# Modulation products summed along rows, and the first part of x ahead of the first weights

## The chip, the cores and the metric

One core of a Trainium2 chip runs the whole program. The metric is the device time of one execution in microseconds (us), the median over runs. TensorE (PE), VectorE (DVE), ScalarE (ACT), GpSimd (POOL) and SyncE (SP) run their own instruction streams and meet only at semaphores. SP and ACT also issue DMAs, each on a queue of its own (q1 is SP's, q10 is ACT's); 16 DMA engines serve both.

## The reference, cut to what matters

Two transformer blocks on 256 tokens of 2048 channels, in fp32. The first is attention, an MLP and a gated embedding. The second is modulated: a vector c (and c_ctx for the context tokens) gives six rows of 2048 that shift, scale and gate its activations.

```python
mod = jax.nn.silu(c) @ w_mod[l] + b_mod[l]          # (2048,) @ (2048, 6 * 2048)
sh_m, sc_m, ga_m, sh_f, sc_f, ga_f = jnp.split(mod, N_MOD)
mod_c = jax.nn.silu(c_ctx) @ w_mod[l] + b_mod[l]     # only its first two parts are used
...
h = modulate(rms_norm_2(x, norm_pre_mix[l]), sh_m, sc_m)    # h * (1 + scale) + shift
```

w_mod is 100 MB; all the other work is matmuls of the 256 tokens with some 490 MB of weights, and attention, a gated scan and convolutions between them.

## The kernel before, in words

**Pieces.** Every weight matrix is cut into pieces of 256 rows by 512 columns, 128 x 1024 in SBUF, 512 KB; there are 940. SP loads a piece into one of four `raw` slots (`load`, L594), ACT rounds it into `whi` (`split`, L695), DVE makes `wlo = raw - whi` (`split`, L1891), and PE does twelve matmuls of 512 columns with it: four each of the tokens' high part with whi, their low part with whi, and their high part with wlo (`chunk`, L1381). Eight pieces are a chunk of 512 output columns (four in two stages). `whi` and `wlo` have four slots each: ACT may split piece p when PE has finished piece p - 4, SP may load into a slot when DVE has made the wlo of the piece that held it. The stages follow one another: "in" (projection, 72 pieces, nine chunks), attention, "o", "ple", "mlp1" (256 pieces), "ctx", "gate", "ctxb", "x2", "gc", "gh", the scan, "pw", "ho", "wo2", "mlp2" (256 pieces).

**Extras.** All other work is put by hand between the pieces: each engine's `chunk` takes a table of extras by slot (0 to 7) of a chunk, and runs an extra before its split of that slot. ACT's and DVE's slots are three pieces ahead of PE. An engine runs its stream in order, so an extra that waits holds the splits behind it.

**Start.** ACT issues the gains and the first part of x (L730 and L731), SP the first piece of weights, then by turns the other three parts of x (`turned_tokens`, L573) and pieces. Each group of x (two of 16 column blocks) is scaled and rounded by ACT (`x_high`, L736) and its low part made by DVE (`x_low`, L1921). PE runs 12 small matmuls on zeros first (`keep_running`, L1448, N_WARM).

**Modulation.** DVE and ACT turn c and c_ctx into silu(c) as columns in `cols`, each value on four partitions (`silu_columns`, L1953, chunk 3 of "in"). Then 192 loads of 512 KB of w_mod come beside the weights (`mod_load`, L631: two DMAs each, into four slots `mraw`), placed by `MOD_PLAN` (L462): 16 in "o", 112 in "mlp1", 32 in "pw" to "wo2", 32 in "mlp2". A load holds 64 rows of w_mod of one part, four partitions to a row. DVE multiplies each half by its column and adds it to `macc` (`mod_product`, L2077; twice where c_ctx counts too). After 32 loads PE transposes `macc` in four 128 x 128 steps (`mod_turn`, L1524; 8 units in all) and DVE sums the result over its free dimension into PSUM (`mod_total`, L2067). `mod_of_mixer`, `other_mods`, `norm4_gain` and `last_mods` add the bias.

**Columns through DRAM.** Where a column vector is wanted as a row on all partitions, ACT writes it to `row_scratch` and reads it back as a broadcast: `lb_columns_out` (L759, chunk 4 of "in", slot 0), `gate_column_out` (L950), and `gate_row_in`, `lb_rows_in` for the reading. In chunks 4 and 5 of "in" SP also loads the attention bias (`two_biases`, L617) in runs of 256 bytes, two DMAs after every piece.

Of the kernel before, what the change touches and what calls it, by code (L numbers as in the profile page):

```python
# [7 lines left out]
ALU = mybir.AluOpType  # L8
# [28 lines left out]
N_WARM = 12  # L37
# [5 lines left out]
        ("norm_post_mix_2", 16), ("norm_post_mlp_2", 16), ("c_2", 64), ("c_ctx_2", 64), ("conv_dw_w_2", 248), ("conv_dw_b_2", 8),  # L43
# [9 lines left out]
ROWS_OF = P // STACK  # L53
# [11 lines left out]
def turned_inputs(a):  # L65

    def by_column(name):
        v = np.asarray(a[name], np.float32).reshape(-1)
        if name in ("c_2", "c_ctx_2"):
            return np.repeat(v.reshape(-1, ROWS_OF).T, STACK, axis=0)  # L70
# [62 lines left out]
def build(nc, I, out):  # L133

    ctx = ExitStack()
    with ctx:
# [50 lines left out]
        c_part = at("c_part", [P, 128], F32, ngain_at)  # L187
# [32 lines left out]
        mraw = at("mraw", [P, MSLOT, 2, NCH], F32, work_at + 40 * K)  # L220
        macc = at("macc", [P, 2, 2, NCH], F32, lev_at)
# [61 lines left out]
        row_scratch = nc.dram_tensor("row_columns", (3, D), F32, kind="Internal").ap()  # L283
        e_scratch = nc.dram_tensor("e_mid", (P, TH, D), F32, kind="Internal").ap()
# [46 lines left out]
        m_red = sem("m_red")  # L331
        m_turned = sem("m_turned")
# [131 lines left out]
        PARTS = [(2, 1), (0, 2), (1, 2), (3, 1), (4, 1), (5, 1)]  # L464
        PART_LOADS = D // (2 * ROWS_OF)
# [26 lines left out]
        MODQ, MOD_AT, SUM_AT, RED_AT = [], {}, {}, {}  # L492
        UNITS, UNIT_END = [], []
        n_ops = 0
        for name, c0, per in MOD_PLAN:
            for a in [8 * (c0 + j) + u for j, count in enumerate(per) for u in AT[count]]:
                m, r = divmod(len(MODQ), PART_LOADS)
                part, nv = PARTS[m]
                MOD_AT.setdefault((name, a // 8), {})[a % 8] = len(MODQ)
                MODQ.append((part, r, m, nv, n_ops))  # L500
                n_ops += 2 * nv
                if r == PART_LOADS - 1:
                    for v in range(nv):
                        at_pe = a + 3 + 2 * v
                        for table, slot in ((SUM_AT, at_pe), (RED_AT, at_pe + 1)):
                            table.setdefault((name, slot // 8), {}).setdefault(slot % 8, []).append(len(UNITS))
                        UNITS.append((m, part, v))
                    UNIT_END.append(len(UNITS))
                    if part == 1:
                        n_ctx_units = len(UNITS)  # L510
            if name == "mlp1":
                n_mlp1_units, n_mlp1_ops, n_mlp1_mods = len(UNITS), n_ops, len(MODQ)
            if name == "mix":
                n_mix_units = len(UNITS)
        assert len(MODQ) == PART_LOADS * len(PARTS)

# [26 lines left out]
        def place(table):  # L543
# [3 lines left out]
            return out  # L547

# [23 lines left out]
        def _(sp):  # L572
# [49 lines left out]

            chunk(w_in, 0, 0, extra={**{u: (lambda u=u: turned_tokens(u + 1)) for u in range(3)}, 6: columns})
# [7 lines left out]
            def mod_load(q):  # L631
                n, r, _, _, _ = MODQ[q]
                if q == n_mlp1_mods:
                    sp.wait_ge(o2_done, NPAIR)
                if q >= MSLOT:
                    done = MODQ[q - MSLOT]
                    sp.wait_ge(m_mul, done[4] + 2 * done[3])
                else:
                    sp.wait_ge(o_lo, NHEAD)
                width = NMOD * D  # L640
# [53 lines left out]
        def _(act):  # L694
# [36 lines left out]
            act.dma_start(xturned[:, 0:2], I["x_turned"][:, 0:2]).then_inc(x_in[0], 16)  # L731
# [19 lines left out]
            def c_exps():  # L751
                act.wait_ge(cols_in, 32)
                nc.scalar.activation(c_part[:], cols[:, COL["c_2"]:COL["c_2"] + 128], ACT.Exp, scale=-1.0).then_inc(c_exp, 1)
# [5 lines left out]
            def lb_columns_out():  # L759
                act.wait_ge(lb_soft, 1)  # L760
                for d in range(2):
                    act.dma_start(row_scratch[2, d * DH:(d + 1) * DH].rearrange("(b p) -> p b", p=P), cols[:, LB0 + 16 * d:LB0 + 16 * d + 8],
                                  allow_slow_non_contiguous=True).then_inc(lb_out, 16)

# [28 lines left out]
            for c in range(IN1 // NCH):  # L793
# [3 lines left out]
                             4: {0: lb_columns_out}}.get(c, {}))  # L797
# [48 lines left out]
            act.dma_start(gbc[:], I["post_mix_norm"][0].partition_broadcast(P)).then_inc(S["gain", "post0"], 16)  # L846
            act.dma_start(pturned[:], I["p_turned"]).then_inc(p_in, 16)
# [91 lines left out]
            mlp("mlp1", 0, True, place({1: high1(3), 2: high1(4), 3: high1(5), 4: high1(6), 5: high1(7), 6: norm1_square,  # L939
# [5 lines left out]
            def lb_rows_in():  # L945
                act.wait_ge(lb_out, 32)
# [17 lines left out]
            def sums_load():  # L964
                act.wait_ge(m_turned, n_mlp1_units)
# [335 lines left out]
            pw_slots = {2: lambda: out_scaled(3), 4: lambda: o2_high(0), 5: lambda: o2_high(1), 7: lambda: o2_high(2), 8: lambda: o2_high(3), 10: lambda: gate_row_in(0, gbc)}  # L1301
# [66 lines left out]
        def _(pe):  # L1368
# [155 lines left out]
            def mod_turn(q):  # L1524
                m, _, v = UNITS[q]
                if q == n_mlp1_units:
                    pe.wait_ge(kt_done, 3 * NPAIR)
                last = MODQ[PART_LOADS * (m + 1) - 1]
                pe.wait_ge(m_mul, last[4] + 2 * last[3])
                if q:  # L1530
                    pe.wait_ge(m_red, q)
# [4 lines left out]
            def sum_inserts(name, c):  # L1536
                return {u: (lambda qs=qs: [mod_turn(q) for q in qs]) for u, qs in SUM_AT.get((name, c), {}).items()}

            p0, g0 = plan["o"]
            for c in range(4):  # L1540
                chunk(p0 + 8 * c, g0 + c, xhi, xlo, inserts=sum_inserts("o", c),
                      tokens={} if c else {u: heads_of(u) for u in range(8)})
# [16 lines left out]
            def mlp(k, u0, extras, first):  # L1559
                p0, g0 = plan[k]  # L1560
                t0 = TG[k][0]
                for i in range(NSB):
                    for j, (kind, c) in enumerate(SEQ):
# [15 lines left out]
                        if k == "mlp2" and n == len(SEQ) * NSB - 1:  # L1579
# [3 lines left out]
                              inserts=merge(extras.get(n, {}), {3: turn_hidden} if j and SEQ[j - 1][0] == "U" else {}, sum_inserts(k, n)),  # L1583
                              tokens=first if n == 0 else {u: hidden(u) for u in range(8)} if kind == "D" and c == 0 else {})
                for f in sum_inserts(k, len(SEQ) * NSB).values():
                    f()
# [264 lines left out]
            for c in range(4):  # L1851
                chunk(p0 + 4 * c, g0 + c, hhi[:, HH:KT], hlo[:, HH:KT], n=4,
                      inserts=merge(slots(ho_slots, 4 * c, 4), mix_slots(SUM_AT, 16 + 4 * c, 4, mod_turn)),
# [7 lines left out]
            chunk(p0, g0, hhi, hlo, inserts=mix_slots(SUM_AT, 32, 8, mod_turn),  # L1861
                  tokens={u: (high_of("y", u), lambda u=u: wo_rest(u)) for u in range(8)})
            for c in range(1, 4):
                chunk(p0 + 8 * c, g0 + c, hhi, hlo, inserts=mix_slots(SUM_AT, 32 + 8 * c, 8, mod_turn))
# [17 lines left out]
        def _(dve):  # L1882
# [70 lines left out]
            def silu_columns():  # L1953
                dve.wait_ge(c_exp, 1)
                cc, ce = cols[:, COL["c_2"]:COL["c_2"] + 128], c_part[:]
# [109 lines left out]
            mps = ps[:, MB, 0:2 * NMOD * KT].rearrange("p (a b) -> p a b", b=2)  # L2065

            def mod_total(q):  # L2067
                _, n, v = UNITS[q]
                dve.wait_ge(m_turned, q + 1)
                to = mps[:, n * KT:(n + 1) * KT, v].rearrange("p (j b) -> p b j", j=STACK)  # L2070
                nc.vector.tensor_reduce(to, ps[:, 7].rearrange("p (b q j) -> p b j q", j=STACK, q=ROWS_OF), AX_X, ALU.add)\
                    .then_inc(m_red, 1)

            def mod_totals(name, c):
                return {u: (lambda qs=qs: [mod_total(q) for q in qs]) for u, qs in RED_AT.get((name, c), {}).items()}

            def mod_product(q):  # L2077
                n, r, m, nv, ops = MODQ[q]
                dve.wait_ge(m_landed[q % MSLOT], 32 * (q // MSLOT + 1))
                if r == 0 and m >= 2:  # L2080

                    dve.wait_ge(m_turned, UNIT_END[m - 2])
                for h in range(2):
                    kt = 2 * r + h
                    for v in range(nv):
                        k = COL["c_2"] + PART_LOADS * 2 * v + kt
                        a, w, x = macc[:, v, m % 2], mraw[:, q % MSLOT, h], cols[:, k:k + 1]
                        if kt == 0:
                            ins = nc.vector.tensor_scalar(a, w, x, None, ALU.mult)
                        else:  # L2090
                            dve.wait_ge(m_mul, ops + nv * (h - 1) + v + 1)
                            ins = nc.vector.scalar_tensor_tensor(out=a, in0=w, scalar=x, in1=a, op0=ALU.mult, op1=ALU.add)  # L2092
# [619 lines left out]
```

## Time and profile before

| | us |
|---|---|
| median of 3 runs | 2819.52 (2816.5 to 2819.88) |
| the profiled execution | 2817.98 |
| its span, first to last instruction | 2816.2 |
| PE busy in the span | 2780.7 (99%) |
| DVE busy | 1996.0 (71%) |
| ACT busy | 1374.8 (49%) |
| DMA, mean over the span | 222 GB/s |

Matmuls are pipelined, so the "mean ns" of one overlaps with the next; the distance from one group of four to the next is what a group costs. Busy time is merged over overlapping instructions. In the profile's rows "<-" after a bracketed time names what ended the idle time before an instruction.

### The profile page before, as it was taken

The numbers are of one execution on the slowest core, as the hardware profiler recorded it, in microseconds if no ns is written. First come the engines' busy times: TensorE is split into PE (matmuls) and PEld (weight loads), VectorE is DVE, ScalarE is ACT, GpSimd is POOL, SyncE is SP. The second block draws the span as 40 slices with busy tenths as digits, with TensorE's granted clock in tenths as the row PEclk, the third lists the DMA queues.
The fourth block names the chain that finished last, engine by engine and source line by source line (L and its number), as shares of the span: only waits on it lengthen the run. The fifth ranks groups of instructions, "written<-read, shape, count | busy, mean of one in ns | idle before, by whom it ended". The sixth has DMA issues, their size and how long they took to land.

```text
span 2816.2 us, 34445 instructions
## 1 busy us (share of the span) xinstructions
PE 2780.7 (99%) x12914; PEld 2312.7 (82%) x12914; DVE 1996.0 (71%) x2265; ACT 1374.8 (49%) x1718; POOL 146.8 (5%) x110
## 2 busy tenths in 40 slices
PE   9999999999999999999999999999989999999998
PEld 7878888888888887788788888898878888888887
DVE  5667877899997676757785488687975467755455
ACT  5446454443444455557444445654564444344443
POOL 0000010010000100000000001000001000010010
PEclk9999999999999999999999999999999999999999
DMA  8963887888888777555666666408856588775654
GB/s 296 208 201 119 278 288 266 276 276 285 284 282 307 255 248 231 194 195 172 216 192 197 197 185 184 133 9 306 304 190 181 193 277 275 255 202 191 190 187 157
DMA packets 332229, 625.23 MB, mean 222 GB/s; under 512 B 36848, under 2 KB 37232, under 8 KB 330224
## 3 DMA queue, kind: packets, MB, share of 16 engines
q1 hardware_dynamic: 323008, 603.41, 67.1%
q10 hardware_dynamic: 9072, 19.83, 2.0%
q8 instruction: 95, 1.56, 0.2%
q14 instruction: 54, 0.44, 0.1%
HBM read 616.83 MB, written 7.27 MB: 222 GB/s over the span
## 4 chain that ended last, share of the span: by engine, by line
PE 91%; DVE 4%; DMA 2%; issue 1%; ACT 1%; SPq 0%; DVEq 0%; POOLq 0%; POOL 0%; ACTq 0%
PE ps L1395 84%; PE ps L1571 1%; DVE wlo L1896 1%; PE ps L1773 1%; DVE macc L2092 1%; PE ps L1374 1%; PE ps L1753 1%; DMA raw<-w_in 1%; DMA raw<-w_o 1%; PE ps L1416 1%; PE ps L1791 1%; PE ps L1496 0%; ACT whi L702 0%; DMA raw<-hgrn_out_w 0%; PE ps L1476 0%
## 5 line engine op out<-in xcount | busy, mean ns | idle before, releaser
L1896 DVE TENSOR_TENSOR wlo<-raw,whi 128x1024 fp32r<-128x1024 f32 x940 | 1169.4, 1250 | 734.2 <-ACT whi L702 729.8
L702 ACT ACTIVATE whi<-raw 128x1024 fp32r<-128x1024 f32 x939 | 994.8, 1060 | 1227.9 <-PE ps L1395 1088.4
L1395 PE MATMUL ps<-whi,hhi 128*128 128x512 f32 x2032 | 549.5, 392 | 0.8 <-DVE yrow L2109 0.8
L1395 PE MATMUL ps<-whi,hlo 128*128 128x512 f32 x2032 | 544.0, 389 | 0.0
L1395 PE MATMUL ps<-wlo,hhi 128*128 128x512 f32 x2032 | 543.4, 389 | 0.5 <-DVE wlo L1896 0.5
L1395 PEld LDWEIGHTS ps<-wlo,hhi 128*128 128x128 f32 x2032 | 381.4, 188 | 80.3 <-DVE wlo L1896 0.9
L1395 PEld LDWEIGHTS ps<-whi,hlo 128*128 128x128 f32 x2032 | 381.1, 188 | 79.6
L1395 PE MATMUL ps<-whi,xhi 128*128 128x512 f32 x1632 | 442.5, 393 | 2.8 <-issue 2.6
L1395 PEld LDWEIGHTS ps<-whi,hhi 128*128 128x128 f32 x2032 | 378.2, 188 | 78.9 <-issue 1.9
L1395 PE MATMUL ps<-whi,xlo 128*128 128x512 f32 x1632 | 439.4, 391 | 0.1
L1395 PE MATMUL ps<-wlo,xhi 128*128 128x512 f32 x1632 | 436.8, 389 | 0.0
L2092 DVE SCALAR_TENSOR_TENSOR macc<-mraw,cols,macc 128x512 f32<-128x512 f32 x504 | 367.3, 760 | 4.6
L1395 PEld LDWEIGHTS ps<-wlo,xhi 128*128 128x128 f32 x1632 | 306.6, 188 | 64.4 <-DVE wlo L1896 0.3
L1395 PEld LDWEIGHTS ps<-whi,xlo 128*128 128x128 f32 x1632 | 306.6, 188 | 64.4 <-DVE xlo L1925 0.5
L1395 PEld LDWEIGHTS ps<-whi,xhi 128*128 128x128 f32 x1632 | 304.3, 189 | 64.8 <-issue 3.2
L2631 POOL TENSOR_TENSOR sqrow<-rrow 128x512 f32<-128x512 f32 x64 | 93.1, 1475 | 1153.6 <-ACT rrow L898 1153.6
L2339 DVE SCALAR_TENSOR_TENSOR yT<-uT,cols,yT 128x252 f32<-128x252 f32 (+17 forms) x144 | 53.1, 437 | 0.0
L2611 POOL TENSOR_TENSOR stat<-stat 128x2 f32<-128x2 f32 x9 | 9.8, 1086 | 656.1 <-DVE stat L2098 441.9
L2157 DVE TENSOR_TENSOR hlo<-ps,hhi 128x512 fp32r<-128x512 f32 x64 | 41.0, 682 | 0.0
L1212 ACT ACTIVATE dec<-ps 128x1024 f32<-128x1024 f32 x32 | 32.5, 1023 | 17.2 <-PE ps L1753 10.8
L1773 PE MATMUL ps<-qD,kD 128*128 128x128 f32 x256 | 34.7, 279 | 3.6 <-DVE qD L2415 2.1
L1773 PEld LDWEIGHTS ps<-qD,kD 128*128 128x128 f32 x256 | 31.0, 192 | 5.1 <-DVE qD L2415 3.1
(303 smaller groups left out, 1470.6 us busy)
## 6 DMA issues: line engine op xcount, KB each, us to landing
raw<-w_in SPq DMA_DIRECT2D x296, 512.0 KB, 4.4
raw<-mlp_w SPq DMA_DIRECT2D x256, 512.0 KB, 4.1
mraw<-w_mod SPq DMA_DIRECT2D x384, 256.0 KB, 5.0
raw<-w_up SPq DMA_DIRECT2D x128, 512.0 KB, 4.7
raw<-w_down SPq DMA_DIRECT2D x128, 512.0 KB, 5.0
raw<-w_o SPq DMA_DIRECT2D x32, 512.0 KB, 5.5
raw<-w_ple_gate SPq DMA_DIRECT2D x32, 512.0 KB, 3.8
raw<-w_out SPq DMA_DIRECT2D x32, 512.0 KB, 5.8
```

The source lines that it names most:

```text
L702: nc.scalar.activation(whi[:, s % NSLOT], raw[:, s % NSLOT], ACT.Copy).then_inc(hi_done, 1)
L1212: nc.scalar.activation(dst, src, ACT.Exp).then_inc(d_done, 1)
L1374: ins = nc.tensor.transpose(ps[:, TB[t % 2], c:c + P], src, ident)
L1395: ins = nc.tensor.matmul(ps[:, bank(par) + th], a[:, kt, th * P:(th + 1) * P], b[:, (s + u) % NSLOT, k], start=(kt == 0 and m == 0), stop= ...
L1416: ins = nc.tensor.matmul(ps[:, bank(g) + th], a[:, kt, th * P:(th + 1) * P], b[:, u % NSLOT, k], start=kt == 0 and m == 0, stop=kt == KT - ...
L1571: ins = nc.tensor.transpose(ps[:, TB[(t0 + h) % 2], a * T + th * P:a * T + (th + 1) * P], sqrow[:, th, f:f + P], ident)
L1773: ins = nc.tensor.matmul(o[:, (2 * hh + n) * P:(2 * hh + n + 1) * P], k[:, hh, n * P:(n + 1) * P], q[:, hh, t * P:(t + 1) * P], start=True ...
L1896: nc.vector.tensor_tensor(wlo[:, s % NSLOT], raw[:, s % NSLOT], whi[:, s % NSLOT].bitcast(F32), ALU.subtract)\
L2092: ins = nc.vector.scalar_tensor_tensor(out=a, in0=w, scalar=x, in1=a, op0=ALU.mult, op1=ALU.add)
L2157: nc.vector.tensor_tensor(hlo[:, kt:kt + 2], ps[:, TB[(t0 + h) % 2]].rearrange("p (a b) -> p a b", a=2), hhi[:, kt:kt + 2].bitcast(F32), A ...
L2339: nc.vector.scalar_tensor_tensor(out=y, in0=tap_part(uT[:, ct], ct, dd, True), scalar=wcol(TAPS // 2 + dd, ct), in1=y, op0=ALU.mult, op1=A ...
L2631: nc.gpsimd.tensor_tensor(sqrow[:, th], rrow[:, th], rrow[:, th], ALU.mult).then_inc(sq_done, 1)
```

## The change

The host passes w_mod transposed (`w_mod_turned`, 12288 x 2048), so a tile holds 128 outputs on the partitions and 1024 of the 2048 inputs along the row. `silu_rows_out` writes silu(c) and silu(c_ctx) from their columns to a DRAM tensor `silu_rows`; `silu_rows_in` broadcasts halves of these rows onto all partitions (`crows`, two slots, exchanged in five phases). DVE's product of a tile with a row is one `tensor_tensor_reduce` whose sum lands in a column of `msum`; the two halves are added later (`mod_parts`). The transposes on PE and the sums of them on DVE are gone. The 192 loads stay at the same places, one DMA each. c and c_ctx come as 16 columns each instead of 64. The first part of x is issued by SP ahead of the first weights, and N_WARM is 11.

```diff
-N_WARM = 12
+N_WARM = 11
...
-        macc = at("macc", [P, 2, 2, NCH], F32, lev_at)
+        mraw = at("mraw", [P, MSLOT, D // 2], F32, work_at + 40 * K)
+        crows = at("crows", [P, 2, D // 2], F32, lev_at)
+        msum = at("msum", [P, 2, (NMOD + 2) * KT], F32, lev_at + 8 * K)
...
+        TILES = [[(2, n, h, 1) for n in range(KT) for h in range(2)],
+                 [(part, n, 0, 2) for part in (0, 1) for n in range(KT)],
+                 [(part, n, 1, 2) for part in (0, 1) for n in range(KT)],
+                 [(3, n, h, 1) for n in range(KT) for h in range(2)],
+                 [(part, n, h, 1) for part in (4, 5) for n in range(KT) for h in range(2)]]
+        CROWS_LOADS = [[(0, 0), (0, 1)], [(1, 0)], [(1, 1), (0, 1)], [(0, 0)], [(0, 0), (0, 1)]]
...  SyncE
+            turned_tokens(0)
             chunk(w_in, 0, 0, extra={**{u: (lambda u=u: turned_tokens(u + 1)) for u in range(3)}, 6: columns})
...
-                for h in range(2):
-                    src = bass.AP(I["w_mod_2"].tensor, ROWS_OF * (2 * r + h) * width + n * D, [[width, ROWS_OF], [NCH, STACK], [1, NCH]])
-                    sp.dma_start(mraw[:, q % MSLOT, h], src).then_inc(m_landed[q % MSLOT], 16)
+                src = I["w_mod_turned"][part * D + n * P:part * D + (n + 1) * P, h * (D // 2):(h + 1) * (D // 2)]
+                sp.dma_start(mraw[:, q % MSLOT], src).then_inc(m_landed[q % MSLOT], 16)
...  ScalarE
-            act.dma_start(xturned[:, 0:2], I["x_turned"][:, 0:2]).then_inc(x_in[0], 16)
...
+            def silu_rows_out():
+                act.wait_ge(silu_done, 1)
+                for v in range(2):
+                    act.dma_start(silu_rows[v].rearrange("(b p) -> p b", p=P), cols[:, COL["c_2"] + v * KT:COL["c_2"] + (v + 1) * KT],
+                                  allow_slow_non_contiguous=True).then_inc(lb_out, 16)
+
+            def silu_rows_in(phase):
+                if phase:
+                    act.wait_ge(m_mul, PHASE_FIRST[phase][1])
+                else:
+                    act.wait_ge(lb_out, 64)
+                for v, h in CROWS_LOADS[phase]:
+                    act.dma_start(crows[:, CROWS_HOLD[phase][v, h]], silu_rows[v, h * (D // 2):(h + 1) * (D // 2)].partition_broadcast(P))\
...
-                             4: {0: lb_columns_out}}.get(c, {}))
+                             4: {0: lb_columns_out, 1: silu_rows_out}}.get(c, {}))
...
             act.dma_start(gbc[:], I["post_mix_norm"][0].partition_broadcast(P)).then_inc(S["gain", "post0"], 16)
+            silu_rows_in(0)
...
+            pw_slots = {1: last_silu_rows, 2: lambda: out_scaled(3), ...
...  TensorE
-            def mod_turn(q):
...
-                for b in range(4):
-                    ins = nc.tensor.transpose(ps[:, 7, b * P:(b + 1) * P], macc[:, v, m % 2, b * P:(b + 1) * P], ident)
-                ins.then_inc(m_turned, 1)
...  VectorE
+                if q == PHASE_FIRST[phase][0]:
+                    dve.wait_ge(crows_in, 16 * sum(len(x) for x in CROWS_LOADS[:phase + 1]))
+                dve.wait_ge(m_landed[q % MSLOT], 16 * (q // MSLOT + 1))
+                w = mraw[:, q % MSLOT]
+                for v in range(nv):
+                    k = (NMOD if v else part) * KT + (part * KT if v else 0) + n
+                    product = w if v == nv - 1 else ps[:, MB:MB + 2].rearrange("p a b -> p (a b)")
+                    if v:
+                        dve.wait_ge(m_mul, ops + v)
+                    nc.vector.tensor_tensor_reduce(out=product, in0=w, in1=crows[:, CROWS_HOLD[phase][v, h]], scale=1.0, scalar=0.0,
+                                                   op0=ALU.mult, op1=ALU.add, accum_out=msum[:, h, k:k + 1]).then_inc(m_mul, 1)
+
+            def mod_parts(dst, a, b, bias):
+                step(nc.vector.tensor_tensor(dst, msum[:, 0, a:b], msum[:, 1, a:b], ALU.add))
+                return nc.vector.tensor_tensor(dst, dst, bias, ALU.add)
```

## Rows read from the trace of the kernel before

**Rows 1.** Busy time by stretch (span, engines, PE clock, DMA share, GB/s).
```profile
0.00:20.00 20.00, 17.78 (x74) 14.41 (x75) 11.04 (x17) 11.68 (x20) 0.57 (x10) 1.00 0.92 331
20.00:210.00 190.00, 188.63 (x845) 155.90 (x844) 118.13 (x133) 91.34 (x104) 8.93 (x5) 1.00 0.84 227
350.00:1070.00 720.00, 720.00 (x3277) 597.60 (x3276) 608.30 (x701) 335.37 (x373) 47.47 (x34) 1.00 0.82 275
1900.00:2005.00 105.00, 104.54 (x488) 86.35 (x487) 87.74 (x97) 45.47 (x59) 1.41 (x1) 1.00 0.87 304
```

**Rows 2.** Waits of PE: who waited for whom, total, times, longest.
```profile
PE ps L1395 <- DVE yrow L2109: 0.8, 1, 0.8
```

**Rows 3.** Groups by line on PE: the transposes of the modulation.
```profile
L1533 PE MATMUL ps<-small,macc 128*128 128x128 f32 x32 | 4.8, 272 | 0.0
```

**Rows 4.** Timeline of PE around one unit: start, duration, instructions.
```profile
1068.98 1.07 PE L1395 MATMUL ps<-whi,hlo 128*128 128x512 f32 x4
1069.88 1.07 PE L1395 MATMUL ps<-wlo,hhi 128*128 128x512 f32 x4
1072.15 1.08 PE L1395 MATMUL ps<-whi,xlo 128*128 128x512 f32 x4
```

**Rows 5.** Groups by line on DVE.
```profile
L2092 DVE SCALAR_TENSOR_TENSOR macc<-mraw,cols,macc 128x512 f32<-128x512 f32 x504 | 367.3, 760 | 4.6
L1932 DVE CUSTOM_DVE_ANT_0 xjunk<-res 128x2048 f32<-128x2048 f32 x1 | 2.3, 2287 | 0.0
```

**Rows 6.** DMA issues of the span: count, KB each, median us to landing.
```profile
gbc<-post_mix_norm ACTq DMA_DIRECT2D x1, 1024.0 KB, 4.6
row_columns<-cols ACTq DMA_DIRECT2D x2, 4.0 KB, 12.1
row_columns<-mcol ACTq DMA_DIRECT2D x2, 8.0 KB, 12.5
```

**Rows 7.** Timeline of the start, ACT and PE.
```profile
6.51 1.71 ACT L740 ACTIVATE xhi<-xturned,cols 128x256 fp32r<-128x256 f32 x4 [3.31 <-DMA xturned<-x_turned]
7.51 1.17 PE L1395 MATMUL ps<-whi,xhi 128*128 128x512 f32 x4 [1.04 <-issue]
14.44 1.06 ACT L702 ACTIVATE whi<-raw 128x1024 fp32r<-128x1024 f32 x1 [2.78 <-DMA raw<-w_in]
16.35 0.77 PEld L1395 LDWEIGHTS ps<-whi,xhi 128*128 128x128 f32 x4 [0.57 <-ACT xhi L740]
17.60 0.77 PEld L1395 LDWEIGHTS ps<-whi,xlo 128*128 128x128 f32 x4 [0.48 <-DVE xlo L1925]
```

**Rows 8.** DMA, 1093 to 1107, in 40 slices; SP's queue: packets, MB, share.
```profile
GB/s 304 117 47 21 7 7 6 0 6 0 0 29 12 18 6 146 29 18 18 53 29 23 29 23 29 35 18 35 35 18 6 41 23 23 59 152 199 228 257 222
q1 hardware_dynamic: 417, 0.80, 54.8%
```

**Rows 9.** DMA, 96 to 108, in 40 slices.
```profile
GB/s 239 198 190 130 137 172 321 333 300 221 170 196 123 70 63 9 0 0 8 0 6 9 16 18 36 6 4 40 37 33 13 36 22 60 76 55 79 180 146 90
```

**Rows 10.** Timeline of ACT in the second MLP.
```profile
2504.84 1.06 ACT L702 ACTIVATE whi<-raw 128x1024 fp32r<-128x1024 f32 x1 [5.79 <-DMA raw<-mlp_w]
```

**Rows 11.** Timeline of ACT in the projection stage.
```profile
95.95 1.03 ACTq L762 DMA_DIRECT2D row_columns<-cols  x2
107.24 1.06 ACT L702 ACTIVATE whi<-raw 128x1024 fp32r<-128x1024 f32 x1 [4.74 <-DMA raw<-w_in]
129.60 1.06 ACT L702 ACTIVATE whi<-raw 128x1024 fp32r<-128x1024 f32 x1 [1.66 <-DMA raw<-w_in]
```

**Rows 12.** Timeline of PE in the projection stage.
```profile
131.11 1.07 PE L1395 MATMUL ps<-whi,xhi 128*128 128x512 f32 x4
```

**Rows 13.** Timeline of PE after a wait.
```profile
1128.41 1.08 PE L1374 MATMUL ps<-small,res 128*128 128x128 f32 x4 [4.34 <-DVE hlo L1914]
1133.84 1.09 PE L1395 MATMUL ps<-whi,xhi 128*128 128x512 f32 x4
```

**Rows 14.** Timeline of SP in the projection stage.
```profile
102.00 8.10 SPq L615 DMA_DIRECT2D bm<-bias_rows  x2
```

More of the change, by code:

```diff
@@ L490, in build @@
         n_pieces = pc[0]
-        MODQ, MOD_AT, SUM_AT, RED_AT = [], {}, {}, {}
-        UNITS, UNIT_END = [], []
+        MODQ, MOD_AT = [], {}
+        PHASE_FIRST, PHASE_AT = [], []
+        order = [(phase, tile) for phase, tiles in enumerate(TILES) for tile in tiles]
         n_ops = 0
@@ L496, in build @@
             for a in [8 * (c0 + j) + u for j, count in enumerate(per) for u in AT[count]]:
-                m, r = divmod(len(MODQ), PART_LOADS)
-                part, nv = PARTS[m]
+                phase, (part, n, h, nv) = order[len(MODQ)]
+                if phase == len(PHASE_FIRST):
+                    PHASE_FIRST.append((len(MODQ), n_ops))
+                    PHASE_AT.append((name, a))
                 MOD_AT.setdefault((name, a // 8), {})[a % 8] = len(MODQ)
[L500 to L510, printed above, removed]
+                MODQ.append((phase, part, n, h, nv, n_ops))
+                n_ops += nv
+                last_at = a
+                if (part, n, h) == (1, KT - 1, 1):
+                    n_ctx_ops = n_ops
+                if len(MODQ) < len(order) and order[len(MODQ)][0] != phase:
+                    PHASE_AT[phase] += (last_at,)
             if name == "mlp1":
-                n_mlp1_units, n_mlp1_ops, n_mlp1_mods = len(UNITS), n_ops, len(MODQ)
+                n_mlp1_ops, n_mlp1_mods = n_ops, len(MODQ)
             if name == "mix":
-                n_mix_units = len(UNITS)
-        assert len(MODQ) == PART_LOADS * len(PARTS)
+                n_mix_ops = n_ops
+        assert len(MODQ) == len(order) and [name for name, *_ in PHASE_AT] == ["o", "mlp1", "mlp1", "mlp1", "mix"]
         TURN_U = 4
@@ L547, in place, with merge_places @@
             return out
+        def merge_places(*tables):
+            return {c: merge(*[place(t).get(c, {}) for t in tables]) for c in {a // 8 for t in tables for a in t}}
         def slots(table, first, n=8):
@@ L631, in mod_load @@
             def mod_load(q):
-                n, r, _, _, _ = MODQ[q]
+                _, part, n, h, _, _ = MODQ[q]
                 if q == n_mlp1_mods:
@@ L1522, in heads_of @@
                 return (lambda: pe.wait_ge(o_hi, n)), (lambda: pe.wait_ge(o_lo, n))
-            def mod_turn(q):
[L1525 to L1531, printed above, removed]
-                for b in range(4):
-                    ins = nc.tensor.transpose(ps[:, 7, b * P:(b + 1) * P], macc[:, v, m % 2, b * P:(b + 1) * P], ident)
-                ins.then_inc(m_turned, 1)
-            def sum_inserts(name, c):
-                return {u: (lambda qs=qs: [mod_turn(q) for q in qs]) for u, qs in SUM_AT.get((name, c), {}).items()}
             p0, g0 = plan["o"]
             for c in range(4):
-                chunk(p0 + 8 * c, g0 + c, xhi, xlo, inserts=sum_inserts("o", c),
-                      tokens={} if c else {u: heads_of(u) for u in range(8)})
+                chunk(p0 + 8 * c, g0 + c, xhi, xlo, tokens={} if c else {u: heads_of(u) for u in range(8)})
             def turn1(g):
@@ L1860, in wo_rest @@
                 pe.wait_ge(t_free, TG["y"][0] + u + 1)
-            chunk(p0, g0, hhi, hlo, inserts=mix_slots(SUM_AT, 32, 8, mod_turn),
-                  tokens={u: (high_of("y", u), lambda u=u: wo_rest(u)) for u in range(8)})
+            chunk(p0, g0, hhi, hlo, tokens={u: (high_of("y", u), lambda u=u: wo_rest(u)) for u in range(8)})
             for c in range(1, 4):
-                chunk(p0 + 8 * c, g0 + c, hhi, hlo, inserts=mix_slots(SUM_AT, 32 + 8 * c, 8, mod_turn))
+                chunk(p0 + 8 * c, g0 + c, hhi, hlo)
             def norm4_turn(g):
@@ L2064, in _ @@
             dve.wait_ge(silu_done, 1)
[L2065 to L2075, printed above, removed]
@@ L2077, in mod_product @@
-            def mod_product(q):
[L2078 to L2092, printed above, removed]
-                        ins.then_inc(m_mul, 1)
+            def mod_product(q):
+                phase, part, n, h, nv, ops = MODQ[q]
+                if q == PHASE_FIRST[phase][0]:
[9 more added lines that the diff above has]
+                                                   op0=ALU.mult, op1=ALU.add, accum_out=msum[:, h, k:k + 1]).then_inc(m_mul, 1)
@@ L2187, in other_mods @@
             def other_mods():
-                for f in mod_totals("mlp1", len(SEQ) * NSB).values():
-                    f()
-                dve.wait_ge(m_red, n_mlp1_units)
-                nc.vector.tensor_tensor(modT[:, NX:NP], mps[:, NX:NP, 0], bmod[:, NX:NP], ALU.add).then_inc(mod_out, 1)
+                dve.wait_ge(m_mul, n_mlp1_ops)
+                mod_parts(modT[:, NX:NP], NX, NP, bmod[:, NX:NP]).then_inc(mod_out, 1)
             def other_gains():
@@ L2198, in norm4_gain @@
             def norm4_gain():
-                dve.wait_ge(m_red, n_mix_units)
-                step(nc.vector.tensor_tensor(modT[:, NP:NM], mps[:, NP:NM, 0], bmod[:, NP:NM], ALU.add))
+                dve.wait_ge(m_mul, n_mix_ops)
+                step(mod_parts(modT[:, NP:NM], NP, NM, bmod[:, NP:NM]))
                 mod_gain(2, 4, 0, "norm_pre_mlp_2")
@@ L2491, in f @@
                             nc.vector.tensor_tensor(add_to[:, :, s], add_to[:, :, s], dst[:, :, s], ALU.add).then_inc(merged, 1)
-                    chunk(p0 + 4 * c, f, n=4, extra=merge(slots(extras, 4 * c, 4), mix_slots(RED_AT, first + 4 * c, 4, mod_total),
+                    chunk(p0 + 4 * c, f, n=4, extra=merge(slots(extras, 4 * c, 4),
                                                           mix_slots(MOD_AT, first + 4 * c, 4, mod_product)))
@@ L2548, in _ @@
             for c in range(4):
-                chunk(p0 + 8 * c, lambda c=c: post3_gain(c), extra=merge(slots(wo_slots, 8 * c), mix_slots(RED_AT, 32 + 8 * c, 8, mod_total),
+                chunk(p0 + 8 * c, lambda c=c: post3_gain(c), extra=merge(slots(wo_slots, 8 * c),
                                                                                              mix_slots(MOD_AT, 32 + 8 * c, 8, mod_product)))
@@ L2556, in last_mods @@
             def last_mods():
-                dve.wait_ge(m_red, len(UNITS))
-                step(nc.vector.tensor_tensor(modT[:, NM:], mps[:, NM:, 0], bmod[:, NM:], ALU.add))
+                dve.wait_ge(m_mul, n_ops)
+                step(mod_parts(modT[:, NM:], NM, NMOD * KT, bmod[:, NM:]))
                 nc.vector.tensor_tensor(mcol[:, 4], modT[:, NM:], col("norm_post_mlp_2"), ALU.mult).then_inc(mcol_done, 1)
@@ L2704 @@
     arrays.update(turned_inputs(arrays))
+    del arrays["w_mod_2"]
     arrays.update(shape_constants())
```

55 lines of the change are left out of this document (27 added, 28 removed).

## The prediction

> **What bounds the kernel now.** I read the table of busy time by stage first: PE is busy 188.63 of 190 us in the projection stage (20 to 210), 720 of 720 in 350 to 1070 and 104.54 of 105 in 1900 to 2005 [rows 1]. The waits of PE come next; the only one near the modulation work is 0.8 us for DVE's last evacuation of the output projection [rows 2]. So PE's own instructions set the end. Time saved on DVE, ACT or SP is worth nothing unless PE waited for it; a PE instruction taken out is worth its own time; and weights that come later than PE's lookahead cost one for one. A piece goes through raw, whi and wlo with four slots each, so ACT splits a piece three pieces before PE uses it. The third reading is therefore DMA: its share is 0.84 in the projection stage, 0.82 in the first MLP and 0.87 in 1900 to 2005 [rows 1].
>
> **Transposes out.** The trace has 32 of them, eight units of four [rows 3]. Four matmuls of 512 columns follow one another at 0.90 us (1068.98 to 1069.88). With one unit between, two such steps took 2.27 us (1069.88 to 1072.15) instead of 1.81 [rows 4]. A unit is worth 0.46 us, eight are worth 3.7 us, all in stages where PE is full: -3.7.
>
> **Products along the row.** DVE now does 504 steps of 760 ns and 8 cheaper first ones. After the change it does 256 multiply-and-sums of 1024 columns. One such over 2048 columns took 2287 ns [rows 5]; half of it, 1.1 to 1.2 us, is my estimate, against 1.5 us for the two steps it replaces, or some 70 us of DVE in all. PE hardly waits for DVE, so this is worth at most the 0.8 us of [rows 2], with nothing as the other end. SP also issues one DMA per load instead of two. I take -0.4, the middle.
>
> **Rows of silu(c) into SBUF.** These are eight broadcasts of 512 KB. A broadcast of 1024 KB landed in 4.6 us [rows 6]. The first two are issued when attention ends, and the first product is a chunk of eight pieces later (8 x 2.72 = 21.8 us, by the step of [rows 4]): no cost. In the first MLP the rows are exchanged three times. ACT issues the load once DVE has finished the products that read the old rows, and the next product is three slots later once and two slots (5.4 us) later twice. There DVE waits perhaps 3 to 6 us for the landing, and behind it in DVE's queue stand the next wlo splits, for which PE waits. PE is three pieces (8.2 us) ahead, so two exchanges should pass; the one that loads two rows at once, with two products per tile after it, may not. Bounds 0 and +4, taken +1, near the lower end since the lookahead covers most. The last two loads (1 MB) come just before the busy stretch at 1900; at its 304 GB/s [rows 1] they are 3.4 us of transfer. Bounds 0 and +3.4; they start before the modulation loads of that stretch, and SP and DVE have less to do there, so I take 0.
>
> **First part of x first.** The first real matmul starts at 7.51 us, and what it waits for is x: ACT was idle 3.31 us for it. But PE then waits again at 16.35 and 17.60, since the fourth piece of weights landed only for the split at 14.44 (ACT idle 2.78 us for it), and the fourth group of x is cast behind that split [rows 7]. The order of the other transfers and their bytes are unchanged, and DMA is full (share 0.92 over the first 20 us, [rows 1]). So PE would start earlier, by 1 us perhaps, and lose it at the fourth piece. Bounds -1 (all of it kept) and +0.5 (one more issue of 0.47 us ahead of that piece); I take 0. One warm-up matmul less lies in the same idle stretch.
>
> **The rows written to DRAM.** This is the term that decides. silu_rows_out writes two vectors, partition by partition: 2048 separate elements of 4 bytes each. The kernel has this shape already: gate_column_out writes one 8 KB vector so, and lb_columns_out two halves of 4 KB. They take 12.5 and 12.1 us to land, where 1024 KB in long runs took 4.6 [rows 6]. What they do to the weights is the point. In the stretch with one 8 KB write, all traffic drops to 26 GB/s on average over 33 slices of 0.35 us (the third to the 35th), 11.5 us, one of them above 60 [rows 8]. In the stretch with the two halves it is 29 GB/s over 24 slices of 0.3 us (the 14th to the 37th), 7.2 us [rows 9]. A 2048-element write thus stops the weights for 7.2 to 11.5 us. Before the change one comes alone: in the second MLP ACT then idles 5.79 us for weights [rows 10] and PE does not wait, as the lookahead takes it.
> After the change three come in a row in the projection stage: lb_columns_out at slot 0 of chunk 4, and two more at slot 1. The first alone uses up the reserve. Issued at 95.95, it makes the split at 107.24 wait 4.74 us, and from there to 129.60 seven pieces come at 3.19 us each, slower than PE's 2.72, because the attention bias is being read in small runs [rows 11]. PE starts on the piece that is split at 129.60 at 131.11 [rows 12]; its split ends at 130.66, so the reserve left is 0.45 us. Two more writes block 2 x 7.2 = 14.4 to 2 x 11.5 = 23 us; middle 19. In that time some 26 GB/s still pass, 0.49 MB, about one piece, worth 3 us. The weights shift by 16, PE stalls by 16 - 0.45 = 15.5. Ends: 14.4 - 3 - 0.5 = +11 and 23 - 3 = +20. After the stop PE must also restart: after one wait of 4.34 us a unit of transposes and twelve matmuls took 5.43 us (1128.41 to 1133.84) instead of 0.46 + 2.72 [rows 13], so 2.2 us; while weights come slower than PE uses them some of this is hidden, taken +1.
> A rule of the Trainium skill speaks against this term. The page "DMA: Bandwidth & Descriptors", section "Queues, rings and completion order", says that each DMA engine takes turns between the queues that have work, a packet at a time. By it the weights on SP's queue would keep every second turn beside ACT's element writes, and the sum would be that of the first rival below. The trace does not agree: the weights' queue moved 0.80 MB in the 14 us of [rows 8].
>
> **Sum.** The profiled execution took 2817.98 us (span 2816.2 and 1.78 around it). 2817.98 - 3.7 - 0.4 + 1 + 0 + 15.5 + 1 = 2831.4, forecast 2831. The median of the three runs shown, 2819.52, lies 1.5 us above the profiled execution; that is inside the range.
>
> **Rivals.**
> (1) The element writes share. The weights keep enough turns beside them, and the lookahead covers the rest as it does in the second MLP [rows 10]. Then the sum without the 15.5 and the restart holds: 2817.98 - 3.7 - 0.4 + 1 = 2814.9, between 2811 and 2818: not slower. It decides if the two added writes together delay the splits by under about half a microsecond, or if they run beside the first at the same total of 12 us. For it: only one case of a lone write with a busy weight queue is shown to cost PE nothing. Against: both GB/s rows.
> (2) ACT is held at the issue. SP once stood 8.10 us over the issue of two small DMAs while the element write ran [rows 14]. If ACT stands likewise behind its first 2048 elements, it can't split pieces that have landed already, raw slots are not freed, and weight loads start late when the block ends: a landing of 4.6 us and one split more, about +7: 2838, 2835 to 2844.
> (3) Half the block. The writes to rows of DRAM overlap each other, and two cost what one costs: 9.5 - 3 - 0.5 = 6 in place of 15.5, so 2822, 2818 to 2825: no measurable change or a little slower.
> (4) The change does not do what it says at the start: the first matmul is not earlier, as x and the first weights now share one queue. It moves the sum by nothing, since the fourth piece decides either way.
>
> **Chances.** Forecast 0.70 (its own range 2825 to 2840), rival 1 0.14, rival 2 0.08, rival 3 0.08. A measurement of this kernel can tell about 0.2% (5.6 us) from no change. Faster by more (under 2813.9): 0.06, less than half of rival 1. Within: 0.17, the rest of rival 1, nearly all of rival 3, and a forecast with every term at its cheap end. Slower: 0.77. The range of 2814 to 2841 leaves out some 0.06 below and 0.08 above.
>
> **What would show it.** Right: in the projection stage PE busy falls by some 15 us, its longest waits there go to wlo or whi and from there to raw<-w_in, DMA's traffic stays under 80 GB/s for some 25 to 30 us from 97 on, the two silu_rows writes land more than 20 us after their issue, and everything behind the stage runs as before, eight units of 0.46 us shorter. The first matmul starts earlier and PE waits longer at the fourth piece. Wrong: the two writes landing within some 12 us of their issue, PE busy all through 95 to 140, or waits of PE on DVE at the exchanges of rows in the first MLP that add up to more than the stage at the start.

## The result, and the profile after

The changed kernel takes 2833.57 us (median of 5 runs, 2832.41 to 2835.08) against 2818.50 us for the kernel before beside it (5 runs, 2816.50 to 2819.88). The ratio is 1.0053, with a 95% interval of 1.0042 to 1.0063: slower by half a percent, which is small but clear of the noise. The profiled execution has a span of 2831.8 us.

Busy time in the first three of the four stretches of [rows 1], now in the changed kernel (columns as there):

```profile
0.00:20.00 20.00, 17.57 (x74) 14.52 (x75) 11.41 (x17) 12.23 (x20) 0.57 (x10) 1.00 0.91 330
20.00:210.00 190.00, 179.22 (x769) 147.30 (x768) 110.32 (x126) 82.39 (x92) 8.03 (x5) 0.96 0.89 212
350.00:1070.00 720.00, 719.75 (x3269) 596.79 (x3268) 586.04 (x707) 338.63 (x384) 56.68 (x35) 1.00 0.82 278
```

Only the projection stage (20 to 210) differs much: PE is busy 179.22 us of 190 instead of 188.63, its clock 0.96 instead of 1.00. The waits of PE name the releaser (total, times, longest):

```profile
PE ps L1420 <- ACT whi L706: 11.2, 3, 5.8
PE ps L1399 <- ACT xs L1362: 6.5, 1, 6.5
PE ps L1399 <- DVE hlo L1920: 4.6, 1, 4.6
```

The second and third line stood in the kernel before too; the first is new, and 10.8 us of it, two waits, lie in the projection stage. ACT's timeline around it (start, duration, instructions, the idle time ahead of them and its releaser) says why the splits are late:

```profile
95.58 1.03 ACTq L765 DMA_DIRECT2D row_columns<-cols  x2
96.74 13.41 ACTq L771 DMA_DIRECT2D silu_rows<-cols  x2
110.25 3.90 ACT L706 ACTIVATE whi<-raw 128x1024 fp32r<-128x1024 f32 x4 [12.46 <-issue]
129.30 1.06 ACT L706 ACTIVATE whi<-raw 128x1024 fp32r<-128x1024 f32 x1 [15.16 <-DMA raw<-w_in]
132.56 1.06 ACT L706 ACTIVATE whi<-raw 128x1024 fp32r<-128x1024 f32 x1 [2.20 <-DMA raw<-w_in]
```

First ACT is held 13.41 us while it issues the two element writes (its idle 12.46 us end with the issue, and four splits follow at once); then it waits 15.16 us for weights. The DMA view of 95 to 137 (40 slices of 1.05 us; then packets, MB and share of the queues of SP and of ACT) shows the stop, and the list of DMA issues the landing:

```profile
GB/s 311 111 257 216 61 12 10 19 27 14 41 89 208 196 52 11 11 4 0 3 22 45 39 35 45 33 62 55 66 26 63 98 140 272 334 219 299 233 262 248
q1 hardware_dynamic: 5564, 4.41, 78.5%
q10 hardware_dynamic: 6208, 0.02, 38.8%
silu_rows<-cols ACTq DMA_DIRECT2D x2, 8.0 KB, 26.3
```

From the fifth slice to the thirty-first, 28 us, three slices are above 80 GB/s: they carry the bytes of about one piece of weights (0.52 MB). Two pieces that were issued at 95.26 and 99.15 land in the stop, 11.9 and 13.0 us later; the next one lands only at 129.3. PE's timeline gives the whole loss, if it is read from start to start, four matmuls being 0.907 us where nothing is late (the groups in between are left out):

```profile
105.35 1.07 PE L1420 MATMUL ps<-wlo,xhi 128*128 128x512 f32 x4
111.36 2.07 PE L1420 MATMUL ps<-whi,xhi 128*128 128x512 f32 x4 [4.94 <-ACT whi L706]
116.25 1.07 PE L1420 MATMUL ps<-whi,xhi 128*128 128x512 f32 x4
123.51 1.07 PE L1420 MATMUL ps<-wlo,xhi 128*128 128x512 f32 x4
130.41 2.08 PE L1420 MATMUL ps<-whi,xhi 128*128 128x512 f32 x4 [5.84 <-ACT whi L706]
136.89 1.07 PE L1420 MATMUL ps<-whi,xlo 128*128 128x512 f32 x4
```

The first wait costs 6.01 - 0.91 = 5.10 us and the slow restart (4.89 us for three groups, instead of 2.72) 2.17; the second wait 6.90 - 0.91 = 5.99 and its restart (6.48 us for four groups instead of 3.63) 2.85. Together 16.1 us. In the slow groups four matmuls take 1.7 to 1.9 us. The granted clock is 0.50, the lower level (1.2 GHz), from 111.4 to 114.9 and from 130.4 to 135.7, behind each wait, and 1.00 from 117 to 123 in between.

Where else the time moved can be read by the start of the same product in each trace against the kernel before (in us; a negative figure is earlier; pieces are counted over the whole program):

| start of | changed | rows in runs (e1) | start alone (e5) |
|---|---|---|---|
| first product | -1.2 | -0.8 | -1.1 |
| piece 8 to 30, projection | -0.4 | 0.0 | 0.0 |
| piece 48, projection | +15.8 | 0.0 | 0.0 |
| first MLP, start | +15.2 | -0.5 | +0.5 |
| context, start | +12.9 | -3.0 | +0.5 |
| after the context products | +13.2 | -4.2 | 0.0 |
| middle of the second block's input | +14.3 | -3.4 | +0.6 |
| after the scan | +16.0 | -2.0 | +2.1 |
| second MLP, piece 5 | +15.8 | -2.3 | +2.4 |
| last product | +15.6 | -2.5 | +2.4 |

The transposes go as forecast. The place of [rows 4] after the change:

```profile
1083.14 1.07 PE L1420 MATMUL ps<-wlo,hhi 128*128 128x512 f32 x4
1084.05 1.07 PE L1420 MATMUL ps<-whi,xhi 128*128 128x512 f32 x4
1084.95 1.07 PE L1420 MATMUL ps<-whi,xlo 128*128 128x512 f32 x4
```

1.81 us from the first to the last, where it was 2.27. DVE's products and its waits for the rows:

```profile
L2082 DVE CUSTOM_DVE_ANT_0 mraw<-mraw,crows 128x1024 f32<-128x1024 f32 x192 | 234.3, 1220 | 3.7 <-DMA crows<-silu_rows 1.4
L2082 DVE CUSTOM_DVE_ANT_0 ps<-mraw,crows 128x1024 f32<-128x1024 f32 x64 | 78.4, 1226 | 4.2 <-DMA crows<-silu_rows 4.2
crows<-silu_rows ACTq DMA_DIRECT2D x8, 512.0 KB, 6.2
```

These are 256 products of 1.22 us, against some 1.5 us for the two steps that each replaces. DVE waited once 4.2 us and once 1.4 us for the rows; no wait of PE names it.

### The profile page after: what moved, and what is told of

It reads as the page before. It is cut to its first block, busy times and chain, and to the rows that moved or that the text cites. A ratio compares the mean times of both kernels' runs of the same rounds, so it can differ in the third digit from the quotient of the medians.

```text
span 2831.8 us, 34002 instructions
## 1 busy us (share of the span) xinstructions
PE 2785.8 (98%) x12880; PEld 2315.1 (82%) x12880; DVE 1948.2 (69%) x2262; ACT 1375.5 (49%) x1718; POOL 154.4 (5%) x110
## 3 DMA queue, kind: packets, MB, share of 16 engines
q1 hardware_dynamic: 295504, 603.61, 66.2%
## 4 chain that ended last, share of the span: by engine, by line
PE 94%; DVE 2%; DMA 1%; ACT 1%; issue 1%; ACTq 0%; SPq 0%; DVEq 0%; POOLq 0%; POOL 0%
PE ps L1420 87%; DMA raw<-w_in 1%; PE ps L1399 1%; PE ps L1580 1%; PE ps L1780 1%; PE ps L1760 1%; PE ps L1441 1%; PE ps L1798 1%; DVE wlo L1902 0%; ACTq L771 0%; PE ps L1521 0%; PE ps L1501 0%; ACT whi L706 0%; DVE cf L2232 0%; PE ps L1634 0%
## 5 line engine op out<-in xcount | busy, mean ns | idle before, releaser
L1420 PE MATMUL ps<-whi,xhi 128*128 128x512 f32 x1632 | 444.8, 395 | 13.7 <-ACT whi L706 10.8
L2082 DVE CUSTOM_DVE_ANT_0 mraw<-mraw,crows 128x1024 f32<-128x1024 f32 x192 | 234.3, 1220 | 3.7 <-DMA crows<-silu_rows 1.4
L2623 POOL TENSOR_TENSOR sqrow<-rrow 128x512 f32<-128x512 f32 x64 | 101.1, 1601 | 1144.1 <-ACT rrow L917 1144.1
L2082 DVE CUSTOM_DVE_ANT_0 ps<-mraw,crows 128x1024 f32<-128x1024 f32 x64 | 78.4, 1226 | 4.2 <-DMA crows<-silu_rows 4.2
L1234 ACT ACTIVATE dec<-ps 128x1024 f32<-128x1024 f32 x32 | 32.5, 1024 | 17.2 <-PE ps L1760 10.8
```

Source lines behind the costliest of these rows:

```text
L1234: nc.scalar.activation(dst, src, ACT.Exp).then_inc(d_done, 1)
L1420: ins = nc.tensor.matmul(ps[:, bank(par) + th], a[:, kt, th * P:(th + 1) * P], b[:, (s + u) % NSLOT, k], start=(kt == 0 and m == 0), stop= ...
L2082: nc.vector.tensor_tensor_reduce(out=product, in0=w, in1=crows[:, CROWS_HOLD[phase][v, h]], scale=1.0, scalar=0.0, op0=ALU.mult, op1=ALU.a ...
L2623: nc.gpsimd.tensor_tensor(sqrow[:, th], rrow[:, th], rrow[:, th], ALU.mult).then_inc(sq_done, 1)
```

## Experiments

The theory: the loss is the two element writes behind lb_columns_out and nothing else. Its rivals: another part of the change; and, within the theory, ScalarE held at the issue instead of weights that don't come. The diffs show the main lines only; "..." stands for arguments that are not printed.

**e1, rows in runs.** The change with one edit: silu(c) is computed in rows, for which SP loads c and c_ctx once more, and written in 32 runs.

```diff
-cc, ce = cols[:, COL["c_2"]:COL["c_2"] + 2 * KT], c_part[:]
+cc, ce = c_rows[0:2 * KT], c_part[0:2 * KT]     # c_2, c_ctx_2 loaded as [16, 128] each
-for v in range(2):
-    act.dma_start(silu_rows[v].rearrange("(b p) -> p b", p=P), cols[...], ...).then_inc(lb_out, 16)
+act.dma_start(silu_rows.rearrange("v (b p) -> (v b) p", p=P), c_rows[0:2 * KT]).then_inc(lb_out, 16)
```

> The change as it stands, but the two silu vectors are held in rows (32 partitions of 128 values) and go to DRAM in one transfer of 32 runs of 512 bytes instead of two transfers of 2048 elements. Theory W (the 16 us of the projection stage are these writes, by what they do to the weights' transfers and to ScalarE together): the step of +16.1 us between pieces 36 and 44 goes, the time is 2817.5 us (2815 to 2820), 16 us under the changed kernel and within 2 us of the one before. Rival R (the step comes from something else that the change put there: the first part of x on SP's queue, the turned weights, the row loads): the time stays above 2828 us and the step stays.

Measured: 2816.91 us against 2817.22, ratio 0.9997 (0.9988 to 1.0007). The step of 16 us is gone, and with it the whole difference. Busy time of 96 to 110 and 110 to 136 in this run, PE full and at full clock:

```profile
96.00:110.00 14.00, 14.00 (x63) 11.61 (x62) 8.35 (x10) 5.23 (x6) 1.18 (x1) 1.00 1.25 119
110.00:136.00 26.00, 26.00 (x116) 21.53 (x115) 15.67 (x18) 10.71 (x11) 1.17 (x1) 1.00 1.07 241
silu_rows<-c_rows ACTq DMA_DIRECT2D x1, 16.0 KB, 13.8
```

By the ratios the two element writes cost 1.0053 - 0.9997, 0.56% or 15.8 us; theory W holds and rival R falls. The interval of e1 itself is -3.4 to +2.0 us; the step is read from the trace.

**e2 and e3, the kernel before with two such writes, and with one.**

```diff
+def probe_rows_out():
+    act.wait_ge(silu_done, 1)
+    for v in range(2):                     # e3: range(1)
+        act.dma_start(probe[v].rearrange("(b p) -> p b", p=P), cols[:, COL["c_2"] + v * KT:...], ...)
-4: {0: lb_columns_out}
+4: {0: lb_columns_out, 1: probe_rows_out}
```

> The kernel before, with nothing added but two writes of 2048 elements each (16 columns of 128 partitions to a spare DRAM tensor that nothing reads) at the place where the changed kernel has its own, right behind the two writes of the lower bound. Theory W: +16 us (+13 to +19), so 2831.5 to 2837.5 us, with a step of the same size between pieces 36 and 44. Rival R: within 3 us of the kernel before.

> The kernel before with one such write instead of two. Under theory W the size tells how the cost grows: if the cost is the elements' share of the transfers' time, half the elements cost about half, +8 us (+6 to +10); if it is a block of which the slots of weights in flight cover the first part, one write costs less than half, +1 to +5 us; if it is ScalarE held while it issues the second write (9.9 us in the changed kernel's trace, against 3.5 us for the first), one write costs 0 to +4 us and ScalarE is held under 4 us.

Measured: e2 2830.17 us, +13.0 (ratio 1.0046, 1.0029 to 1.0062), just below what was expected (+13 to +19 us, or 2831.5 us and more); its trace has a step of 12.8 us between pieces 30 and 44. e3 2824.17 us, +7.0 (1.0022, 1.0012 to 1.0032). So half the elements cost about half. In e3 ScalarE is held 2.88 us only, and yet PE waits, for weights that have not landed (ACT's timeline):

```profile
97.64 2.88 ACTq L770 DMA_DIRECT2D probe<-cols  x1
114.51 1.06 ACT L704 ACTIVATE whi<-raw 128x1024 fp32r<-128x1024 f32 x1 [6.59 <-DMA raw<-w_in]
122.16 1.06 ACT L704 ACTIVATE whi<-raw 128x1024 fp32r<-128x1024 f32 x1 [6.59 <-DMA raw<-w_in]
```

Why two writes cost 12.8 us in e2's trace and 16.1 in the changed kernel's is open. In both, ACT makes four splits between its hold and the long wait. In e2 the writes land sooner (median 23.5 us behind their issue, 26.3 in the changed kernel) and the second wait costs 4.5 us instead of 6.0; the restarts cost 3.2 us instead of 5.0, at a mean granted clock of 0.87 from 110 to 136 instead of 0.76.

**e4, the writes issued by GpSimd.** The same two writes move from ACT's queue to GpSimd's, behind `pool.wait_ge(hi_done, 36)`, so that they start at nearly the same time (issued at 98.99, in the change at 96.74):

```diff
-4: {0: lb_columns_out, 1: silu_rows_out}
+4: {0: lb_columns_out}
+for v in range(2):
+    pool.dma_start(silu_rows[v].rearrange("(b p) -> p b", p=P), cols[...], ...).then_inc(silu_out, 16)
```

> The changed kernel with the two writes issued by GpSimd, which has nothing to do in that stage, instead of ScalarE, at the same time. Theory W1 (the weights are starved by the element writes on the shared transfer engines): the cost stays, 2827 to 2834 us, and PE waits for weights that landed late. Theory W2 (ScalarE, held 13.4 us at the issue, can't split the weights that have landed): the cost goes, 2816 to 2821 us, though the elements are still moved in the same stretch.

Measured: 2833.76 us, ratio 1.0051 (1.0035 to 1.0068), the same as the change. ACT is not held at all; it waits for weights, and PE once for ACT (ACT's timeline, then PE's):

```profile
131.03 1.06 ACT L707 ACTIVATE whi<-raw 128x1024 fp32r<-128x1024 f32 x1 [18.65 <-DMA raw<-w_in]
132.14 2.07 PE L1416 MATMUL ps<-whi,xhi 128*128 128x512 f32 x4 [14.23 <-ACT whi L707]
```

The hold of 13.41 us in the changed kernel thus is not a second price: theory W1. It decides only where PE waits, once for 14.23 us here and twice for 4.94 and 5.84 us there.

**e5, the start alone**, on the kernel before: x part 0 on SP's queue ahead of the first weights, N_WARM 11.

```diff
-act.dma_start(xturned[:, 0:2], I["x_turned"][:, 0:2]).then_inc(x_in[0], 16)
+turned_tokens(0)                            # on SP, ahead of the first chunk
```

> The kernel before with the start of the change alone: the first part of x on SP's queue ahead of the first weights, and 11 warming groups instead of 12. The prediction's term: 0 (-1 to +0.5 us). By the trace of the changed kernel the first product starts 1.2 us earlier, and from the fourth piece on 0.3 us are left, since the third weights land no earlier (14.1 us against 14.4): same time as before within the measurement, first product near 6.3 us and piece 4 within 0.5 us of the kernel before. Rival (the start holds and is worth 1.2 us): piece 4 and all later ones 1.2 us earlier.

Measured: 2818.06 us against 2818.37, ratio 1.0000 (0.9991 to 1.0009). PE starts at 6.40 us and loses the gain at the fourth piece (timelines of PE and ACT):

```profile
6.40 1.36 PE L1395 MATMUL ps<-whi,xhi 128*128 128x512 f32 x4 [0.36 <-DVE whi L1961]
16.32 1.19 PE L1395 MATMUL ps<-whi,xhi 128*128 128x512 f32 x4 [1.30 <-ACT xhi L740]
14.41 1.06 ACT L703 ACTIVATE whi<-raw 128x1024 fp32r<-128x1024 f32 x1 [2.79 <-DMA raw<-w_in]
```

The weights land for 14.41, as before (14.44 in [rows 7]). This run also sizes the noise of a single trace: behind the start it is the kernel before, and its products still drift by +2.4 us, in steps at the scan (+1.6) and at the start of the second MLP (+1.0) that the changed kernel's column has too (+1.7, and +0.5 where a unit of transposes goes as well).

**e6 and e8, the change's writes elsewhere.** In e6 they stand at pieces 52 and 64, in e8 both at piece 52; the lower bound's writes and the bias loads have landed by then.

```diff
-4: {0: lb_columns_out, 1: silu_rows_out}
+4: {0: lb_columns_out}, 6: {4: lambda: silu_row_out(0)}, 8: {0: lambda: silu_row_out(1)}   # e6
+4: {0: lb_columns_out}, 6: {4: silu_rows_out}                                              # e8
```

> The changed kernel with its two element writes apart and away from the others: one at piece 52 and one at piece 64 of the projection, after the lower bound's writes and the bias loads have landed. Theory S (each write of 2048 elements takes its share from the weights, about 7 us, wherever it stands): 2829 to 2833 us, with a step of 6 to 7 us behind each. Theory C (the weights in flight and the slots cover one write of 2048 elements, as they cover the lower bound's in the kernel before; only what comes on top of it and of the bias loads is paid): 2816 to 2819 us and no step over 1.5 us.

> The changed kernel with both element writes at piece 52, one right behind the other as in the change, but after the lower bound's writes and the bias loads. It asks what the company of the writes has to be for the block. Theory C1 (a number of elements together: the cover holds for 2048 and what comes on top is paid at about 6.5 us for 2048): 2821 to 2825 us, a step of 5 to 8 us in the eight pieces behind piece 52. Theory C2 (the bias loads on SP's queue, which stand among the weights in small runs, are needed too): 2815 to 2818 us and a step under 2 us. ScalarE should be held at the issue of the second write by about 10 us under both.

Measured: e6 2814.73 us against 2818.37 (0.9989, 0.9980 to 0.9998), 1.3 us below the expected band. Its trace has a step of 0.6 us behind the first write (issued at 148.52) and none behind the second (184.06): the cover takes a lone write. Another 0.6 us come from 125 to 138, ahead of both. e8 2826.04 us against 2818.65 (1.0027, 1.0016 to 1.0037), 1 us above the expected band, with a step of 8.7 us: 4096 elements together are too many without the bias loads too, theory C1, though the price of what comes on top is above its 6.5 us. The hold was expected at 10 us in e8 and did not come:

```profile
147.91 1.92 ACTq L771 DMA_DIRECT2D silu_rows<-cols  x2
163.86 1.06 ACT L706 ACTIVATE whi<-raw 128x1024 fp32r<-128x1024 f32 x1 [9.48 <-DMA raw<-w_in]
171.44 1.06 ACT L706 ACTIVATE whi<-raw 128x1024 fp32r<-128x1024 f32 x1 [6.52 <-DMA raw<-w_in]
```

Two writes are issued in 1.92 us where the queue is empty. In the change they were the third and fourth on ACT's queue, and the issue of the fourth waited.

**e7, a better version.** e1, and the kernel's own element write in the context stage moved ahead of the scan:

```diff
-5: lb_rows_in, 8: lambda: gate_column_out(0, 3), 12: embedding_in,
+5: lb_rows_in, 12: embedding_in,
                           held=1 if n and c == 3 else 0)
+gate_column_out(0, 3)
```

> The version with the silu vectors written in runs, and one more element write moved: the gate's 2048 elements, which ScalarE writes in the context stage beside 2 MB of other loads, go behind the two convolution gates' weights, ahead of the scan, where few transfers run. If the wait of 4.3 us and the slow restart at about 1124 us are this write's cost [as the rows of the kernel before suggest], 6.5 us go: 2810.5 us (2809 to 2813), faster than both kernels. If they belong to the loads beside it, the wait stays and the time is 2816 to 2819 us. If the write only moves its cost, a new wait stands near 1800 to 1810 us.

Measured: 2810.79 us against 2818.37, ratio 0.9977 (0.9967 to 0.9986), faster than both kernels. PE's wait in the context stage ([rows 13]: 4.34 us) is now 0.65, and no new one stands before the scan:

```profile
1121.86 0.63 PE L1403 MATMUL ps<-small,res 128*128 128x128 f32 x4 [0.65 <-DVE hlo L1924]
1122.24 1.17 PE L1424 MATMUL ps<-whi,xhi 128*128 128x512 f32 x4
```

## Why the prediction was right

**Rows written to DRAM: +15.5 and +1 for the restart, measured 16.1.** The place and the cause, element writes that stop the weights, are the forecast ones, shown by e1 and e2. The split between the two terms was not: the waits are 11.1 us and the restarts 5.0, one too high by 4.4 and the other too low by 4.0, so that the sum fits this well by luck. In e4, with one wait, they are 14.4 and 2.7. The changed kernel has two waits because ACT was held: the piece that PE waited for until 111.36 had been issued at 89.82 and had landed 5.3 us later, but ACT split it only when its issue ended. So of the prediction's signs one held by half (only the second wait goes back to raw<-w_in), and PE's busy time fell by 9.4 us, not 15, since the slow matmuls of the restarts count as busy. A single write after the lower bound's costs 7.0 (e3); by the prediction's own figures it is 7.2 to 11.5, less half a piece that passes (1.5) and the reserve (0.5), so 5.2 to 9.5.

**Rival 1, sharing, falls** in e2 and e3, but its reserve is real: where one write stands alone the prediction's "lookahead takes it" holds (e6). **Rival 3, half the block, falls** in e2 against e3: 13.0 is not 7.0. **Rival 2, ACT held at the issue,** was half right: the hold occurred, 13.41 us, landed pieces stayed unsplit and SP issued the next weights late. But it added nothing. SP's timelines give the issue of the piece that ends the long wait, in the changed kernel and in e4, where ACT was free:

```profile
112.59 0.37 SPq L603 DMA_DIRECT2D raw<-w_in  x1
103.75 1.62 SPq L604 DMA_DIRECT2D raw<-w_in  x1
```

It lands 16.7 us later in the one and 27.3 in the other: at 129.3 and 131.0. Issued 9 us earlier, it came no sooner. **Rival 4** falls: the first product is 1.2 us earlier.

**Transposes: -3.7.** A unit is 0.46 us as forecast. Between the start of the first MLP and that of the context stage, column e1 moves by 2.5 us; steps of 0.46, 0.94 and 0.93 us in the first MLP, five units, make 2.3 of it. By time the rest of the change is worth -0.8 us (e1, interval -3.4 to +2.0) to -3.1 (e6, -5.6 to -0.6), where the prediction's other terms sum to -3.1.

**Rows of silu(c) into SBUF: +1, measured 0.** DVE was late once by 4.2 us, at the exchange that loads two rows, as forecast; PE's lookahead took it. **Start: 0,** shown by e5's trace (0.0 from piece 8 on); its time tells it only to 2.5 us. **DVE: -0.4,** not resolved: e1 is 0.5 us earlier at the start of the first MLP, but e5, with DVE's old work, is 0.5 later there.

**The rule on turns between queues.** The prediction said that the trace disagrees with it, and that was more than the rows bore. In e6, from 153 to 161, the queues' rows (packets, MB, share of 16 engines) are these:

```profile
q1 hardware_dynamic: 122, 0.25, 64.2%
q10 hardware_dynamic: 151, 0.00, 5.9%
```

The weights' queue does have the larger share of the engines' time; what is slow is each of its packets: 64.2% of 16 x 8 us for 122 packets are 0.67 us each, against 0.10 over the whole changed kernel (66.2% of 16 x 2831.8 us for 295504 packets).

```profile
q1 hardware_dynamic: 295504, 603.61, 66.2%
```

So the Trainium skill's rule ("DMA: Bandwidth & Descriptors", "Queues, rings and completion order") may hold here and still not save the weights. No run here shows whether the queues take turns. Another rule of the Trainium skill bears on the fix ("DMA: Bandwidth & Descriptors", "Rules for kernel authors"): a strided last dimension becomes one descriptor per element, and should be rearranged to be contiguous. The trace agrees: ACT's queue moved 6208 packets from 95 to 137 in the changed kernel, 2048 of the lower bound's and 4096 of the two writes among them; in e1 it was 2128. On GpSimd's queue it can't be read so: in e4 the same two writes stand in the trace as 96 packets, and cost as much.

## What to carry to other kernels

A transfer like this is priced by its elements, not its bytes: here 16 KB written as 4096 single values cost 16 us of the critical path, and written in 32 runs nothing that shows. Count the element writes that are in flight together against the lookahead of the stream that they stand beside: in this kernel one of 2048 is covered and each further one beside it cost 6 to 9 us (e2, e3, e8), so spread them, write rows, or move them to a stretch without loads. Moving such writes to GpSimd's queue changed nothing.

## What the runs showed of the hardware

The stop outlasts most of the element packets: in e6 ACT's queue moved 2064 packets from 148 to 163 but only 151 of them after 153, while the weights stayed at 31 GB/s until 161. It ended when the write landed, 12.3 us after its issue, at 160.8, and so it did in e3 (97.64 + 20.9 = 118.5). In e8 it ended at 170, and the second write landed only at 176. What the engines wait for isn't in the records. GpSimd's queue took the same writes in an issue of 2.52 us, with the same harm. ACT's issue of a fourth element write was held 9.9 us (10.5 in e2), of a third 2.9 to 3.5 us; the first two took 1.03 to 1.92 us together. e1's write in 32 runs, a third one as well, took 3.37 us to issue, so it may be the place on the queue that counts.
